# A gather of experts on one core: the first group's picks chosen in two halves, and four queries and a group's scores placed between value products

## What is computed

```python
q = (hb @ w_query).reshape(PEER_TOKEN_BLOCK, PEER_HEADS, 2, half)
s = jnp.einsum("thpd,hpnd->thpn", q, sub_keys).astype(jnp.float32)
s_top, i_top = lax.top_k(s, PEER_TOPK)
cand = (s_top[:, :, 0, :, None] + s_top[:, :, 1, None, :]).reshape(
    PEER_TOKEN_BLOCK, PEER_HEADS, PEER_TOPK * PEER_TOPK)
...
best, pos = lax.top_k(cand, PEER_TOPK)
expert = jnp.take_along_axis(cand_idx, pos, axis=-1)
gate = jax.nn.softmax(best, axis=-1)
u = jnp.take(u_tab, expert, axis=0)
act = jax.nn.gelu(jnp.einsum("thkd,td->thk", u, hb).astype(jnp.float32), approximate=False)
w = (gate * act).astype(hb.dtype)
return jnp.einsum("thk,thkd->td", w, jnp.take(v_tab, expert, axis=0))
```

## Time and profile before

| | |
|---|---|
| median of three runs | 2832.18 us (2830.0 to 2835.06) |
| profiled execution, its own time | 2834.92 us |
| its span | 2833.1 us |
| mean granted TensorE clock | 0.855 |
| busy: PE, DVE, ACT, POOL | 77%, 69%, 45%, 24% |
| bytes moved by DMA | 846.90 MB, mean 299 GB/s |
| of it the software queue (POOL's) | 579.38 MB |
| picks | 512 (L990), first issue at 310.0 us, last at 1702.4 us |
| POOL idle ahead of L990 | 679.2 us for PE's products (L1990), 97.6 us for expert numbers (L2627) |

### The profile page before, as it was taken

How to read it: one execution, slowest core, us unless ns; L and a number is a source line. 1 busy time by engine, 2 the same in 40 slices (tenths; PEclk the granted TensorE clock), 3 DMA queues, 4 the chain that set the end, 5 groups by cost and what they waited for, 6 DMA issues and landing times. The chain is left out here.

```text
span 2833.1 us, 39427 instructions
## 1 busy us (share of the span) xinstructions
PE 2173.3 (77%) x12874; PEld 1497.9 (53%) x12874; DVE 1968.9 (69%) x4290; ACT 1261.3 (45%) x3045; POOL 667.1 (24%) x599
## 2 busy tenths in 40 slices
PE   7998866444586678766444446999999999999998
PEld 4545733111364546444211104888668878885787
DVE  2885576777687567865667766778657777775777
ACT  3365323332466346642233324446454454563544
POOL 1410344445334333433444450000000000000000
PEclk9999877555797889888655557999999999999999
DMA  9954899999999999999999995665246656552564
GB/s 347 398 213 165 308 419 421 421 421 421 420 407 401 416 417 415 406 419 418 421 421 421 421 421 217 190 186 161 82 135 188 188 158 188 174 165 62 169 187 148
DMA packets 156746, 846.90 MB, mean 299 GB/s; under 512 B 17329, under 2 KB 17457, under 8 KB 90161
## 3 DMA queue, kind: packets, MB, share of 16 engines
q0 software_dynamic: 85392, 579.38, 49.8%
q1 hardware_dynamic: 69584, 253.86, 27.8%
q10 hardware_dynamic: 1616, 11.69, 1.2%
HBM read 843.80 MB, written 1.05 MB: 298 GB/s over the span
## 5 line engine op out<-in xcount | busy, mean ns | idle before, releaser
L2650 DVE SCALAR_TENSOR_TENSOR arena<-arena 128x1024 f32<-128x1024 f32 x308 | 373.5, 1225 | 195.2 <-DMA arena<-experts,arena 191.2
L1936 PE MATMUL ps<-a_both,w_hi 128*128 128x512 f32 x1408 | 503.0, 400 | 5.8 <-DVEq L2405 2.7
L990 POOL DMA_INDIRECT arena<-experts,arena x308 | 366.2, 1189 | 563.2 <-PE ps L1990 420.5
L1990 PE MATMUL ps<-arena 128*32 128x512 f32 x1232 | 237.4, 858 | 337.8 <-ACT arena L1302 327.7
L1063 ACT ACTIVATE w_hi<-weights 128x512 fp32r<-128x512 f32 x528 | 334.2, 634 | 361.3 <-PE ps L1938 267.8
L2386 DVE TENSOR_TENSOR w_lo<-weights,w_hi 128x512 fp32r<-128x512 f32 x528 | 356.6, 690 | 164.8 <-ACT w_hi L1063 153.2
L1938 PE MATMUL ps<-a_both,w_lo 128*128 128x256 f32 x1408 | 395.7, 281 | 0.0
L1296 ACT ACTIVATE arena<-arena 128x1 f32<-128x1 f32 x512 | 102.1, 199 | 576.7 <-DVE arena L2650 328.9
L1990 PE MATMUL ps<-held,arena 128*32 128x512 f32 x816 | 157.2, 855 | 217.0 <-ACT arena L1302 206.7
L2650 DVE SCALAR_TENSOR_TENSOR held<-held,arena 128x1024 f32<-128x1024 f32 x204 | 247.2, 1224 | 109.9 <-DMA held<-experts,arena 107.0
L990 POOL DMA_INDIRECT held<-experts,arena x204 | 248.3, 1217 | 307.4 <-PE ps L1990 258.8
(11 more groups left out here) (291 smaller groups left out, 3677.9 us busy)
## 6 DMA issues: line engine op xcount, KB each, us to landing
weights<-stream SPq DMA_DIRECT2D x445, 512.0 KB
arena<-mod_rows_in POOLq DMA_DIRECT2D x67, 512.0 KB, 8.4
mod_rows<-mod_rows_in POOLq DMA_DIRECT2D x13, 512.0 KB, 7.4
arena<-experts,arena POOLq DMA_INDIRECT x308
held<-ada_in SPq DMA_DIRECT2D x8, 512.0 KB, 11.9
arena<-ada_in SPq DMA_DIRECT2D x8, 512.0 KB, 15.5
held<-kept_in SPq DMA_DIRECT2D x1, 4096.0 KB, 13.1
arena<-kept_in SPq DMA_DIRECT2D x8, 512.0 KB, 7.3
```

Source lines behind the costliest of these rows:

```text
L990: pool.indirect_dma_start(out=pair_of(k), out_offset=None, in_=experts[k // PICKS], in_offset=bass.IndirectOffsetOnAxis(ap=expert[:, at:at ...
L1936: pe.matmul(dst, w_hi[:, o % 2, cut], a_both[:, :, k, :], start=(k == 0), stop=False, skip_group_check=True)
L1990: ins = pe.matmul(ps[first:first + WAVE, v % 2, :], diag[:, one % DIAGS, :], v_of(one, HALF * half, HALF * (half + 1)), start=(k % WAVE_PI ...
L2650: dve.scalar_tensor_tensor(out=u, in0=u, scalar=1.0, in1=h_rows[:, v % 2, :], op0=ALU.mult, op1=ALU.mult, accum_out=act_raw[:, at:at + 1]) ...
```

## The change

Four edits.

1. The choice of group 0 has five parts, all at beat -1: part 0 as before; part 1 the sums and only their top 8 (`top8`); part 2 the expert numbers of these 8 (`place(at, 0, 8)`), which raises `expert_ready`; part 3 the sums again (`place` has overwritten them), the second 8 (`second8`) and the logits; part 4 the expert numbers 8 to 15, which raises `expert_ready` again. All other groups keep three parts.
2. POOL waits for the first signal at pick 0, for the second at pick 8, and for every later group for a count that is one higher; ACT's `scores` wait for the same higher count.
3. Queries 12 and 13 of the first half of the tokens move from beat -1 to beat 1 on PE and ACT, queries 14 and 15 to beat 3.
4. Scores 1 move with them to beat 3, on PE and ACT. The choice of group 1 stays at DVE's beats 4, 5 and 6.

```diff
+FIRST_QUERY_BEATS = {12: 1, 13: 1, 14: 3, 15: 3}
+EARLY_PICKS = 8
...
     for m in range(2 * H):
-        put("query", 0, 0, m, pe=-1, act=-1)
+        beat = FIRST_QUERY_BEATS.get(m, -1)
+        put("query", 0, 0, m, pe=beat, act=beat)
         if m == 2 * GROUP_HEADS - 1:
             put("scores", 0, pe=-1, act=-1)
             put("rows", 0, pe=-1, act=-1)
-            for part in range(3):
+            for part in range(5):
                 put("choose", 0, part, dve=-1)
...
-    put("scores", 1, pe=-1, act=-1)
+    put("scores", 1, pe=beat, act=beat)
...
-                    if k % TOPK == 0:
-                        pool.wait_ge(expert_ready, k // TOPK + 1)
+                    if k == 0:
+                        pool.wait_ge(expert_ready, 1)
+                    elif k == EARLY_PICKS or k % TOPK == 0:
+                        pool.wait_ge(expert_ready, k // TOPK + 2)
...
-                        act.wait_ge(expert_ready, c - 1)
+                        act.wait_ge(expert_ready, c)
...
+                def place(at, first, end):
+
+                    n = end - first
+                    a_u, a_f = ab_u[:, :, first:end], ab_f[:, :, first:end]
+                    hits, got = eq[:, :, first:end], pick[:, :, first:end]
+                    dve.tensor_scalar(a_u[:, 0], best_p[:, first:end], 4, None, ALU.logical_shift_right)
+                    link(dve.tensor_scalar(a_u[:, 1], best_p[:, first:end], 15, None, ALU.bitwise_and))
+                    link(dve.tensor_copy(a_f, a_u))
+                    link(dve.tensor_tensor(hits, const("iota", a=0, b=TOPK).unsqueeze(1).unsqueeze(1).to_broadcast([P, 2, n, TOPK]),
+                                           a_f.unsqueeze(3).to_broadcast([P, 2, n, TOPK]), ALU.is_equal))
+                    link(dve.tensor_tensor(hits, hits, top_f.unsqueeze(2).to_broadcast([P, 2, n, TOPK]), ALU.mult))
+                    link(dve.reduce_sum(got, hits, AX_X))
+                    dve.scalar_tensor_tensor(out=expert[:, TOPK * at + first:TOPK * at + end], in0=got[:, 0],
+                                             scalar=float(NKEY), in1=got[:, 1], op0=ALU.mult,
+                                             op1=ALU.add).then_inc(expert_ready, 1)
...
+                    elif c == 0 and part == 1:
+                        pairs_of_keys()
+                        link(top8([(cand, cand2, best, best_p)]))
+                    elif c == 0 and part == 2:
+                        place(at, 0, EARLY_PICKS)
+                    elif c == 0 and part == 3:
+                        pairs_of_keys()
+                        second8([(cand, cand2, best, best_p)])
+                        logits(at)
+                    elif part == 1:
+                        pairs_of_keys()
                         top16([(cand, cand2, best, best_p)])
...
+                        logits(at)
+                    else:
+                        place(at, EARLY_PICKS if c == 0 else 0, TOPK)
```

More of the change, by code:

```diff
@@ L2584, in normed, with top8 @@
                                       ALU.mult).then_inc(normed_ready, 1)
-                def top16(rows):
+                def top8(rows):
                     for values, scratch, top, index in rows:
@@ L2591, in top16, with second8 @@
                     for values, scratch, top, index in rows:
-                        dve.max_index(index[:, 0:8], top[:, 0:8], values)
+                        ins = dve.max_index(index[:, 0:8], top[:, 0:8], values)
+                    return ins
+                def top16(rows):
+                    top8(rows)
+                    second8(rows)
+                def second8(rows):
                     for values, scratch, top, index in rows:
@@ L2601, in top16, with pairs_of_keys, logits @@
                     link(ins)
+                def place(at, first, end):
[12 more added lines that the diff above has]
+                                             op1=ALU.add).then_inc(expert_ready, 1)
+                def pairs_of_keys():
+                    dve.tensor_copy(top_f, top_i)
+                    link(dve.tensor_tensor(cand.rearrange("p (i j) -> p i j", i=TOPK),
+                                           top_v[:, 0, :].unsqueeze(2).to_broadcast([P, TOPK, TOPK]),
+                                           top_v[:, 1, :].unsqueeze(1).to_broadcast([P, TOPK, TOPK]), ALU.add))
+                def logits(at):
+                    dve.tensor_tensor(gate[:, TOPK * at:TOPK * (at + 1)], best, best[:, 0:1].to_broadcast([P, TOPK]),
+                                      ALU.subtract).then_inc(logits_ready, 1)
                 def choose(c, part):
@@ L2607, in choose @@
                         top16([(score[:, c % 2, e, :], score2[:, e, :], top_v[:, e, :], top_i[:, e, :]) for e in range(2)])
[L2608 to L2613, removed]
-                        top16([(cand, cand2, best, best_p)])
-                        dve.tensor_tensor(gate[:, TOPK * at:TOPK * (at + 1)], best, best[:, 0:1].to_broadcast([P, TOPK]),
-                                          ALU.subtract).then_inc(logits_ready, 1)
-                        return
@@ L2618, in choose @@
[L2618 to L2629, removed]
+                    elif c == 0 and part == 1:
[9 more added lines that the diff above has]
+                        pairs_of_keys()
+                        top16([(cand, cand2, best, best_p)])
+                        logits(at)
+                    else:
+                        place(at, EARLY_PICKS if c == 0 else 0, TOPK)
```

## The result

| | kernel before | changed kernel |
|---|---|---|
| median | 2834.92 us (9 runs, 2830.0 to 2837.24) | 2840.02 us (9 runs, 2833.74 to 2844.08) |
| ratio | 1 | 1.0023, 95% interval 1.0015 to 1.0032 |
| profiled execution, its span | 2833.1 us | 2838.2 us |
| first MAX8 of group 0 (DVE) | 301.04 us | 300.66 us |
| span behind that MAX8 | 2532.1 us | 2537.5 us |

The change made the kernel slower by 0.23%, 6.5 us (interval 4.3 to 9.1), where 3.6 to 3.8 was forecast and "no change that can be measured" was thought likeliest (0.70, against 0.27 for slower). The forecast of 2836.0 us counts from 2832.18, the median of three runs; that of nine is 2.7 us higher, so the comparison goes by the ratio.

The account below looks back on a forecast made before the run. Gather stage bound by transfers, its time changed by gaps: -2.3 and -1.5 gained, +3.7 and +3.5 lost, +0.2 added, sum +3.6; from the median 2832.18 this gives 2836.0 us, range 2828.0 to 2840.5.

Parts of the forecast that it names:

- Step 1: Choice of group 0 on DVE: first issue moves from 310.05 to about 307.8 us, worth 2.28 us.
- Step 2: Thin place at 335 to 340 us: earlier first product lets POOL issue pick 10 at 329.0, worth 1.5 us.
- Step 3: PE and ACT queues: scores 1 stand behind products, so the second choice starts on DVE at 341.1, 8.5 us later.
- Step 4: Gather: picks 14 and 16 issued at 348.3 and 356.8; two gaps cost 3.7 and 3.5 us, 0.2 added.
- Rival A: Gather start: only the gains, if second choice at most about 4 us late; 2828.4 us; 0.20 with half ways and C.
- Rival B: PE at low clock for the second pair and query 14: +6.3 us, 2838.5, up to 2840; chance 0.25.
- C: Thin places covered by other traffic, so start alone counts or nothing: 2830 to 2832 us; 0.20 shared with Rival A.

Follow-up runs that it names:

- early_only: Changed kernel with queries 12 to 15 and scores 1 put back to beat -1, leaving the two signals alone; ratio to the kernel before 0.9998.
- moved_only: Kernel before with queries 12 to 15 and scores 1 moved to beats 1 and 3, without the two signals; ratio 1.0021.
- two_queries_only: Changed kernel with queries 12 and 13 back at beat -1, and 14, 15 and scores 1 at beat 1; ratio to the kernel before 1.0001.
- choice_at_7: Changed kernel with the choice of group 1 in one piece at DVE's beat 7 instead of from beat 4; ratio to the kernel before 1.0000.
- four_queries_choice_7_late_8: Changed kernel with choice 1 in one piece at DVE's beat 7 and late squares, norm and shift five beats later; ratio to the kernel before 1.0009.
- half_dots_5_to_20: Changed kernel with dots of picks 5 to 20 over the first 512 of 1024 columns only; one run, 2833.16 us.
- two_queries_choice_7_late_8: Changed kernel with only queries 14, 15 and scores 1 moved (beat 1), choice 1 whole at beat 7, late norm five beats later; ratios to before 0.9989, 0.9997.

## Why the prediction was off

*Step 1, the early start: right.* First issue 6.72 us behind the MAX8 against 9.01 before, 2.29 less (2.28 forecast). The repeated pair sums and the later logits cost nothing.

*Step 2, the thin place: right in kind, too large.* Pick 10 was issued at 327.84 (329.0 forecast), and 335 to 340 is full. The first pair ran in 1.07 us, not 1.93. Together the two gave 3.0 us of transfer, where 3.8 was written: the thin place of the kernel before was 349 GB/s over 5 us in the earlier trace rows, 0.9 us of transfer, and not the 1.5 us read from its dots. The prediction says of the early start that it counts only "if the flow behind it is kept up"; early_only shows it. What neither step says is that both gains are gone as soon as the transfers run dry once: moved_only.

*Step 3, the late scores: right, by luck in one place.* MAX8 at 340.80 (341.1), DVE idle 13.15 us in front of it. On the way there two misses cancelled. The first pair ran at full clock, 0.9 us shorter than forecast. The low clock came behind it: PE had been idle for 2.94 us ahead of that pair, the granted clock was 1.00 in 326 to 328 and 0.51 in 328 to 331 (1.2 GHz), and queries 12 and 13 took 5.46 us where 4.15 was forecast. They ended at 332.97 (332.9 forecast).

*Step 4, the order of events: right.* Pick 14 at 347.95 (348.3), pick 16 at 356.84 (356.8), two holes. moved_only, two_queries_only, choice_at_7 and four_queries_choice_7_late_8 show that this chain is the cause and in which order its holders stand.

*Step 4, the price: this is the step that failed, and the term is the pace behind a fresh start.* The sum goes up to the dot of pick 16, adds 0.2 us because "the first picks of a start are not yet at the pace of the flow", and then lets the picks come 2.49 us apart. Counted from the mark, against the kernel before:

| | forecast | measured |
|---|---|---|
| dot of pick 16 later by | 3.5 us | 4.2 us |
| dot of pick 17 | 3.6 | 4.8 |
| dot of pick 20 | 3.6 | 5.6 |
| picks 20 to 300, median | 3.6 | 5.8 |

- Up to pick 16 the forecast missed 0.7 us. Of it 0.4 are the issue, which lay where it was forecast although the first MAX8 of this trace was 0.4 us earlier. The rest is the fresh start: by the profile's landings pick 14 took 6.4 us and pick 16 6.2 us from issue to landing, where 5.97 was taken from pick 0. The longer issues (1.91 and 1.50 us beside a dot) put the start of the data off by 0.8 us and more, but most of this does not show in the landing.
- Behind pick 16 it missed 1.4 us: 1.6 measured (from 4.2 to 5.8), 0.2 written. A start puts off more than its first pick. Dot 17 waited for its landing and came 3.06 us behind dot 16 (2.49 before), and by dot 20 the delay had grown by 0.7 us more. It is nearly the same where pick 16 started afresh in other kernels: from dot 16 to picks 20 to 300 the delay grew by 1.7 us in moved_only, 1.2 in choice_at_7 and 1.3 in half_dots_5_to_20. In the last one issues 17 to 19 took 0.94 us each, in the changed kernel 1.99, so the long issues are the smaller part of it (0.3 us between these two). That the second pick of a start comes late could be read before: dots 0 and 1 are 3.49 us apart in the kernel before (316.02 and 319.51, where other work of DVE ended just ahead), and 4.52 in the changed kernel, where dot 1 waited for its landing (317.66). Part of it is that a start moves little at first: 197 GB/s in 359 to 360, with all engines busy. What sets this no run shows.

```profile
319.51 1.23 DVE L2650 SCALAR_TENSOR_TENSOR arena<-arena 128x1024 f32<-128x1024 f32 x1 [0.15 <-issue]
```

The transfers tell the same in another cut: 4.8 us in the first hole (3.7 forecast), 3.5 in the second (3.5), 0.9 behind it (0.2), and 3.0 gained ahead of them (3.8); net 6.2, against 5.8 by the dots and 6.5 by the ratio. The first hole is larger at the transfers because they thin out before the last landing: 0.20 of the engines' time was used in 346 to 347, while pick 13, by the profile, landed at 349.0. A dot starts when all sixteen increments of its pick have come.

*Rival A* (only the gains, decided at a second choice at most 4 us late) did not come. two_queries_only had the second choice 5.8 us late and its ratio was 1.0001 (0.9992 to 1.0011), so this condition (4 us) was not tested. Its other one, dots 5 and 7 free of the wait, is choice_at_7: pick 16 was issued 6.2 us later than before even so. *Rival B* named the size that came (+5.7 and more, 0.25) but not its mechanism: behind a pause of 1.46 us the pair before query 14 ran in 1.06 us, at full clock, and queries 14 and 15 took 3.84 us for 3.66. *C* did not come. The estimate of 4.4 us for a fresh start that the Trainium skill gives ("DMA: Bandwidth & Descriptors", Anatomy of one DMA) would have made the miss larger. The trace does not agree with it: from the first issue to its dot it is 5.8 to 6.1 us in all traces.

What stays open: choice_at_7 and two_queries_only have ratios of 1.0000 and 1.0001 with 2 to 3 us to either side, and picks 20 to 300 are 3.2 and 3.1 us later than before. The trace of these picks says slower by 3 us; the total times can't confirm it.

## What to carry to other kernels

Where a stage is bound by transfers, find the first buffer that is given back and the last wait that gives it: moving an issue earlier was worth nothing (early_only) as long as the issue behind the stock of buffers did not move too. And before a step is put behind work of its own consumers, ask what is queued behind it on every in-order engine: here four queries moved by two pairs cost the second choice 8.6 us, and a wait placed ahead of three dots on DVE carried this into two picks. When a hole opens, price more than the first transfer of the new start: the picks right behind it still come further apart than in full flow (1.6 us more behind pick 16 here). Such a price can be read at the start of the stage, from the second and third transfer.

## What the runs showed of the hardware

- POOL's indirect DMA mostly takes 0.94 us when no dot of DVE is under way. When one is, and has 0.2 to 1.15 us to go, the issue takes the rest of that dot plus 0.80 to 0.83 us, in all 181 such issues of the kernel before (0.79 to 0.82 in 172 of the changed one), so up to 1.99 us. A dot that starts behind the issue seldom matters: 17 of 161 such issues took over 1.1 us, and 3 of the 70 that met no dot. With dots half as long the longest issue of picks 14 to 20 was 1.38 us. The Trainium skill, "SBUF — State Buffer", SBUF: two separate sides, has a DVE operation with two SBUF inputs contend with a GpSimd operation that reads SBUF, the loser blocked to the end of the other's instruction. The dot has two such inputs and the gather reads its row numbers from SBUF; the trace agrees.
- Behind a fresh start the dot of the second gather came 3.5 to 4.6 us behind that of the first (dots 0 and 1 in all twelve traces; in the changed kernel 4.52, with dot 1 waiting for its landing), where the flow has 2.49.
- The phases ahead of the gather stage vary by 10 us from execution to execution for the same instructions (first MAX8 at 296.15 in one, 306.29 in another). Of one kernel traced twice (two_queries_choice_7_late_8) the totals lie 7.8 us apart, the first MAX8 5.2, the span behind it 2.6, the dots of picks 20 to 300 0.5. So the dots behind a mark told these kernels apart far better than a total time.
